# All norms of a two-block decoder kernel: reciprocal roots as one GpSimd power in place of a ScalarE, VectorE chain

## The chip, the cores and the metric

The kernel runs on one core of one Trainium2 chip. The metric is the device time of one execution in microseconds. TensorE does the matmuls, VectorE and ScalarE the elementwise work, GpSimd (called POOL in the profile) a few elementwise operations and some of the DMAs, SyncE the stream of weight loads.

## What is computed

A batch of 256 positions of width 2048 runs through two layers of a first model and two of a second. The part that matters here is how often a norm occurs:

```
for layer in range(2):                       # first block
    u = rmsnorm(h, norm_g[layer, 0])
    m = even_mixer(u) if layer == 0 else nsa_mixer(u)
    h = h + rmsnorm(m, norm_g[layer, 1])
    u = rmsnorm(h, norm_g[layer, 2])
    h = h + rmsnorm(swiglu(u), norm_g[layer, 3])
for layer in range(2):                       # second block
    h = rmsnorm(x, norm_g_2[layer])
    ...                                      # dilated + MoBA, then differential + stick-breaking
    x = x + y @ w_out[layer]
return rmsnorm(x, final_norm_g_2)
```

Each rmsnorm multiplies by (mean of squares + 1e-6) to the power -0.5. The even mixer has more: an L2 norm of the heads of q and k after a short convolution, and an rmsnorm of the heads of its two outputs. The differential attention has one on its output.

## The kernel before

The work has six stages, numbered 0 to 5: even mixer, SwiGLU, NSA mixer, SwiGLU, and the two layers of the second block. The 256 positions are two tiles of 128 partitions (t = 0, 1). Each weight is streamed from HBM in slots of 256 x 512 or 128 x 1024 elements, split by ScalarE into a high part (L1531, `WH`) and by VectorE into a low part (L1998, `WL`), and multiplied by TensorE three times (L1013 to L1015 for the columns of an input projection, L1060 to L1062 for the rows of an output projection). Three buffers hold split slots, so the split runs at most some slots ahead of TensorE.

All engines walk one list of steps, `ORDER`, written by `write_order`, and each engine does its own part of a step: `prep` is the split of a slot, `sq` and `stat` are sums of squares, `pre` is the norm ahead of a stage (its result `HR` scales what is drained from PSUM), `root` the norm of a stage's output (its result `MR` goes into `new_h`), `cv_r` and `cv_n` the L2 norm after the convolution, `og_r` and `og_m` the norm at the output gate of the even mixer, `y2d` that of the differential attention, `fin_s` and `fin_y` the last norm. An engine works its steps strictly in the order of the list: a step that waits holds all behind it on that engine.

A root is made by the helper `rstd`, which is in both the ScalarE and the VectorE program: VectorE writes x = mean + eps (L2005), ScalarE takes the square root (L1536), VectorE takes the reciprocal and one Newton step (L2007, L2009, L2011, L2013) and writes the result (L2015). The results lie in 24 columns each of a ring `RSQ`. The square root needs a table that most other functions don't share, so the compiler puts a table load ahead of a root and another ahead of the next function; a step `warm` (L1574) loads the table early, at the start of the second half of an output projection.

GpSimd's list has, besides elementwise steps, these DMAs, which matter below:

- `gb`: the row of gains of the coming output norm.
- `cm_w(0)` (L2595): the first half of the NSA compression weights, 2 MB, put in the list after the last step of stage 1's crossing into stage 2; it waits for the end of stage 1's matmuls alone. TensorE's `cm_h` (L1310) reads it.
- `tables_n` (L2586 to L2590): five tables of stage 2, about 1 MB. VectorE's and GpSimd's `cm_b` (L2280, L2604) wait for the last one and make the operand of `cm_h`.
- `tables_2` (L2621 to L2623): seven tables for stages 4 and 5, which wait for the residual stream of stage 4. Behind them stand a small operation (L2625), which waits for the last table, and `gb(4)`; then `rope` (L2633, L2634, L2637 on GpSimd, L2366, L2367, L2370 on VectorE), whose output TensorE's `feat` (L1407) reads.

`pre(2)` and `pre(4)` are put in the list by `cross`, ahead of these DMAs:

```
    ffn(1)              # ends with cross(1), which puts pre(2)
    put("cm_w", 0)
    put("tables_n")
    ...
    ffn(3)              # ends with cross(3), which puts pre(4)
    put("tables_2")
    put("gb", 4)
```

Of the kernel before, what the change touches and what calls it, by code (L numbers as in the profile page):

```python
# [21 lines left out]
EPS = 1e-6  # L22
# [221 lines left out]
def write_order(slots):  # L244
# [462 lines left out]
def build(nc, A, out):  # L707
    with ExitStack() as ctx:
# [30 lines left out]
        RSQ = sb("RSQ", 8 * 24)[:]  # L739
# [14 lines left out]
        one_b = SM[:, 30:31]  # L754

# [131 lines left out]
        rs_index = {}  # L887

        def rstd_of(w, *key):

            j = rs_index.setdefault(key, len(rs_index))
            before = [k for k, n in rs_index.items() if n == j - 8]
            return [RSQ[:, 24 * (j % 8) + 8 * i:24 * (j % 8) + 8 * i + w] for i in range(3)], before

# [14 lines left out]
        def slot_of(s):  # L909
# [3 lines left out]
            if wd < 64:  # L913
# [7 lines left out]
        a_hi, a_ut, a_ff, a_z, a_nm, a_gd, a_cv, a_hg, a_og, a_ns, a_b2, a_rs = (  # L921
            steps("s_act_" + n, act) for n in ("weights", "operand", "ffn", "sink", "norm", "gdn", "conv", "hgrn",
                                               "gate", "nsa", "block2", "root"))
# [3 lines left out]
        g_nm, g_gd, g_hg, g_og, g_ns, g_b2 = (  # L927
            steps("s_pool_" + n, pool) for n in ("norm", "gdn", "hgrn", "gate", "nsa", "block2"))
# [587 lines left out]
        def scalar(e):  # L1516
# [452 lines left out]
            def fin_s(t):  # L1969
# [17 lines left out]
        def vector(e):  # L1987
# [73 lines left out]
            def mul(st, c, t):  # L2061
# [3 lines left out]
                on.wait_ge(*v_rs.of("r", "pre", st))  # L2065
# [169 lines left out]
            def og_m(a, hf):  # L2235
                on.wait_ge(*v_rs.of("r", "og", a, hf))
# [203 lines left out]
            def y2d(i):  # L2440
# [7 lines left out]
                on.wait_ge(*v_rs.last())  # L2448
# [24 lines left out]
            def fin_y(t):  # L2473
                on.wait_ge(*v_rs.of("r", "pre", 6, t))
# [10 lines left out]
        def gpsimd(e):  # L2485
# [4 lines left out]


# [162 lines left out]
            def y2d(i):  # L2654
# [3 lines left out]
                e.tensor_tensor(sq, y, y, ALU.mult).then_inc(*g_b2.inc("sq", i))  # L2658
                on.wait_ge(*v_b2.of("yn", i))
# [109 lines left out]
```

## Time and profile before

| | us |
|---|---|
| median of 3 runs | 2965.33 |
| lowest and highest run | 2959.11, 2966.28 |
| the profiled execution | 2962.29 |
| its span, first to last instruction | 2960.5 |
| TensorE busy in the span | 2841.2 |
| VectorE busy | 1613.4 |
| ScalarE busy | 1402.6 |
| GpSimd busy | 234.6 |

The span is 1.8 us shorter than the execution's time. TensorE's busy time covers 96% of the span; its idle time, and the stretches in which the granted clock is at half, are all that a change off TensorE can alter. In rows of the timeline the numbers are start and duration in us, then engine, line, operation, tiles (out<-in) and form; in brackets stands how long the engine was idle ahead of the row and who ended that.

### The profile page before, as it was taken

To read this page: it belongs to the slowest core of one execution; us is meant where nothing else is said; L and a number is where in the kernel's file an instruction comes from. 1 tells how busy PE (TensorE), PEld (TensorE's weight loads), DVE (VectorE), ACT (ScalarE), POOL (GpSimd) and SP (SyncE) were. 2 spreads that over 40 slices of the span, in tenths; PEclk is the share of its full clock that TensorE was granted. 3 is DMA by queue.
4 is the path that set the end of the run, shared out by engine and by line. 5 is a ranking of instruction groups with operands and counts; after the bars stand their busy time and mean duration, and the time that the engine had idled before them with its cause. 6 is when DMAs were issued, how large, how long until landed. Compare 5 with 4: busy or idle time off the path is not lost.

```text
span 2960.5 us, 33218 instructions
## 1 busy us (share of the span) xinstructions
PE 2841.2 (96%) x13558; PEld 2346.8 (79%) x13558; DVE 1613.4 (54%) x2004; ACT 1402.6 (47%) x2045; POOL 234.6 (8%) x209
## 2 busy tenths in 40 slices
PE   8899999999999999999999999999999999999986
PEld 6787887777888888888888877788888888877765
DVE  5664666756554554444645545655455444476655
ACT  6554345546444444344544444644444434465563
POOL 0112332300000000000100101000000000011112
PEclk9999999999999999999999999999999999999998
DMA  6654543656666666555664423666666655554422
GB/s 211 123 115 120 106 106 85 122 180 192 185 192 191 185 191 191 187 191 190 192 190 138 140 95 129 191 185 192 191 185 190 191 188 191 190 182 143 135 93 99
DMA packets 212776, 480.85 MB, mean 162 GB/s; under 512 B 15248, under 2 KB 16272, under 8 KB 211984
## 3 DMA queue, kind: packets, MB, share of 16 engines
q1 hardware_dynamic: 210272, 467.57, 54.4%
q0 software_dynamic: 2352, 11.17, 1.1%
q8 instruction: 106, 1.74, 0.2%
q14 instruction: 46, 0.38, 0.0%
HBM read 476.58 MB, written 2.10 MB: 162 GB/s over the span
## 4 chain that ended last, share of the span: by engine, by line
PE 82%; DVE 8%; ACT 6%; issue 1%; POOL 1%; DMA 1%; SPq 0%; DVEq 0%; ACTq 0%; POOLq 0%
PE PS L1013 17%; PE PS L1015 17%; PE PS L1014 17%; PE PS L1062 7%; PE PS L1061 7%; PE PS L1060 7%; DVE WL L1998 2%; ACT WH L1531 1%; DVE WORK L2139 1%; PE PS L1171 1%; DVE XL L1998 1%; PE PS L1270 1%; PE PS L1359 1%; PE PS L1259 1%; PE PS L1086 1%
## 5 line engine op out<-in xcount | busy, mean ns | idle before, releaser
L1998 DVE TENSOR_TENSOR WL<-RAW,WH 128x1024 fp32r<-128x1024 f32 x827 | 1028.4, 1246 | 943.3 <-ACT WH L1531 942.3
L1531 ACT ACTIVATE WH<-RAW 128x1024 fp32r<-128x1024 f32 x831 | 874.5, 1054 | 849.3 <-PE PS L1015 524.0
L1013 PE MATMUL PS<-WH,UTH 128*128 128x512 f32 x2396 | 965.5, 403 | 25.0 <-DVE WL L1998 22.4
L1015 PE MATMUL PS<-WH,UTL 128*128 128x512 f32 x2396 | 939.9, 392 | 0.0
L1014 PE MATMUL PS<-WL,UTH 128*128 128x512 f32 x2396 | 939.3, 392 | 0.0
L1013 PEld LDWEIGHTS PS<-WH,UTH 128*128 128x128 f32 x2396 | 454.0, 189 | 124.7 <-DVE WL L1998 26.3
L1015 PEld LDWEIGHTS PS<-WH,UTL 128*128 128x128 f32 x2396 | 453.2, 189 | 98.4
L1014 PEld LDWEIGHTS PS<-WL,UTH 128*128 128x128 f32 x2396 | 454.4, 190 | 89.9 <-issue 1.9
L1062 PE MATMUL PS<-WH,HTL 128*128 128x512 f32 x656 | 259.3, 395 | 0.0
L1061 PE MATMUL PS<-WL,HTH 128*128 128x512 f32 x656 | 258.8, 394 | 0.0
L1060 PE MATMUL PS<-WH,HTH 128*128 128x512 f32 x656 | 255.4, 389 | 0.0
L1060 PEld LDWEIGHTS PS<-WH,HTH 128*128 128x128 f32 x656 | 125.3, 191 | 28.0
L1061 PEld LDWEIGHTS PS<-WL,HTH 128*128 128x128 f32 x656 | 123.2, 188 | 27.6
L1062 PEld LDWEIGHTS PS<-WH,HTL 128*128 128x128 f32 x656 | 123.2, 188 | 25.6
L1060 PE MATMUL PS<-WH,UTH 128*128 128x512 f32 x256 | 107.2, 419 | 4.1 <-DVE UTL L2041 4.0
L1061 PE MATMUL PS<-WL,UTH 128*128 128x512 f32 x256 | 103.9, 406 | 0.0
L1062 PE MATMUL PS<-WH,UTL 128*128 128x512 f32 x256 | 103.7, 405 | 0.0
L1998 DVE TENSOR_TENSOR XL<-RAW,XH 128x1024 fp32r<-128x1024 f32 x53 | 63.9, 1220 | 16.9 <-ACT XH L1531 16.9
L1580 ACT ACTIVATE BIG<-PS,SM 128x512 f32<-128x512 f32 x68 | 42.9, 683 | 51.0 <-PE PS L1015 50.7
L1552 ACT ACTIVATE UTH<-PS,GP 128x128 fp32r<-128x128 f32 x160 | 46.2, 386 | 41.8 <-PE PS L992 41.8
L1531 ACT ACTIVATE XH<-RAW 128x1024 fp32r<-128x1024 f32 x53 | 55.2, 1066 | 20.6 <-DMA RAW<-in_ffn_w_down 8.5
L1060 PEld LDWEIGHTS PS<-WH,UTH 128*128 128x128 f32 x256 | 50.9, 199 | 16.0 <-issue 3.2
(424 smaller groups left out, 2612.2 us busy)
## 6 DMA issues: line engine op xcount, KB each, us to landing
RAW<-in_ffn_w_gu SPq DMA_DIRECT2D x352, 512.0 KB, 4.2
RAW<-in_ffn_w_down SPq DMA_DIRECT2D x176, 512.0 KB, 4.4
RAW<-in_ab_w_in SPq DMA_DIRECT2D x128, 512.0 KB, 4.7
RAW<-in_nsa_w_in SPq DMA_DIRECT2D x80, 512.0 KB, 3.7
RAW<-in_w_in SPq DMA_DIRECT2D x64, 512.0 KB, 3.9
RAW<-in_ab_w_out SPq DMA_DIRECT2D x32, 512.0 KB, 4.4
RAW<-in_nsa_w_out SPq DMA_DIRECT2D x32, 512.0 KB, 3.8
RAW<-in_w_out SPq DMA_DIRECT2D x16, 512.0 KB, 3.8
```

Of the source, the lines that this page charges most:

```text
L1013: e.matmul(o, lh, wh[:, j], start=k + j == 0, stop=False)
L1014: e.matmul(o, lh, wl[:, j], start=False, stop=False)
L1015: x = e.matmul(o, ll, wh[:, j], start=False, stop=k + j == NKT - 1)
L1060: e.matmul(o, lh, wh[:, 0, cs], start=k == (0 if hf else LEFT[st][0]), stop=False)
L1061: e.matmul(o, lh, wl[:, 0, cs], start=False, stop=False)
L1062: x = e.matmul(o, ll, wh[:, 0, cs], start=False, stop=k == (KTILES[st] - 1 if hf else LEFT[st][-1]))
L1086: x = e.transpose(b[:, 128 * j:128 * j + 128], g[:, 128 * j:128 * j + 128], ident)
L1171: x = e.matmul(b[:, 128 * h:128 * h + 128], LTM[:, h], XX[:, h, 0], start=True, stop=True)
L1531: e.activation(wh, raw, ACTF.Copy).then_inc(*a_hi.inc(s))
L1552: e.activation(UTH[:, kk, 128 * t:128 * t + 128], b[:, 128 * j:128 * j + 128], ACTF.Copy, scale=GP[:, st, kk:kk + 1]).then_inc(*a_ut.inc(" ...
L1580: e.activation(dst, banks.ap("acc", st, c, t)[:, 0:WIDTHS[st][c]], ACTF.Copy, scale=HR[:, t:t + 1]).then_inc(*banks.empty(a_z, "acc", st, ...
L1998: e.tensor_tensor(wl, raw, wh.bitcast(F32), ALU.subtract).then_inc(*v_lo.inc(s))
```

## The change

`rstd` is gone from ScalarE. On VectorE it is one operation, which writes x over the sum itself, with the gain folded in. GpSimd raises it in place to the power -0.5, read from eight columns of constants (`MHALF`). The consumers wait for GpSimd's semaphore. GpSimd thereby gets the steps `pre`, `root`, `cv_r`, `og_r` and `fin_s`, and one operation in `y2d`; it does them where they stand in the list. The steps `warm` and the ring `RSQ` go away.

```diff
@@ right(st)
-        put("warm", "rows", st)
@@ scalar
-            def rstd(w, *key):
-                (x, y, z), before = rstd_of(w, *key)
-                on.wait_ge(*v_rs.of("x", *key))
-                e.activation(y, x, ACTF.Sqrt).then_inc(*a_rs.inc(*key))
...
-            @step
-            def pre(st):
-                rstd(2, "pre", st)
...
             def sink(dst, st, c, t, col):
                 on.wait_ge(*p_mm.of(col_end[st, c]))
-                on.wait_ge(*v_rs.of("r", "pre", st))
+                on.wait_ge(*g_rs.of("r", "pre", st))
@@ vector
             def rstd(o, ss, n, gain, *key):
-                (x, y, z), before = rstd_of(ss.shape[1], *key)
-                if before:
-                    on.wait_ge(*v_rs.of("r", *before[0]))
-                e.tensor_scalar(x, ss, 1.0 / n, EPS, ALU.mult, ALU.add).then_inc(*v_rs.inc("x", *key))
-                on.wait_ge(*a_rs.of(*key))
-                e.reciprocal(y, y).then_inc(*v_rs.inc("y", *key))
-                on.wait_ge(*v_rs.last())
-                e.tensor_tensor(z, y, y, ALU.mult).then_inc(*v_rs.inc("yy", *key))
-                on.wait_ge(*v_rs.last())
-                e.tensor_tensor(z, z, x, ALU.mult).then_inc(*v_rs.inc("xyy", *key))
-                on.wait_ge(*v_rs.last())
-                e.tensor_scalar(z, z, -0.5 * gain, 1.5 * gain, ALU.mult, ALU.add).then_inc(*v_rs.inc("z", *key))
-                on.wait_ge(*v_rs.last())
-                e.tensor_tensor(o, y, z, ALU.mult).then_inc(*v_rs.inc("r", *key))
+                e.tensor_scalar(o, ss, 1.0 / (n * gain * gain), EPS / (gain * gain), ALU.mult,
+                                ALU.add).then_inc(*v_rs.inc("x", *key))
...
             def new_h(st, t, n):
-                    on.wait_ge(*v_rs.of("r", "post", st, t))
+                    on.wait_ge(*g_rs.of("r", "post", st, t))
@@ gpsimd
+            def root_of(o, *key):
+                on.wait_ge(*v_rs.of("x", *key))
+                e.tensor_tensor(o, o, MHALF[:, 0:o.shape[1]], ALU.pow).then_inc(*g_rs.inc("r", *key))
+
+            @step
+            def pre(st):
+                root_of(HR, "pre", st)
...
             def y2d(i):
                 e.tensor_tensor(sq, y, y, ALU.mult).then_inc(*g_b2.inc("sq", i))
+                root_of(ST2[:, 64 + 4 * i:68 + 4 * i], "y2d", i)
                 on.wait_ge(*v_b2.of("yn", i))
```

The order of instructions shows what moves. GpSimd at the crossing from stage 1 to stage 2, before (the first row is `gb(1)`, the second `cm_w(0)`, the rest `tables_n` and the first of `cm_b`):

```order
L2508 DMA WORK<-in_norm_g 128x2048 [waits s_dve_norm]
L2595 DMA BIG<-in_nsa_cmp_w 128x32x128 [waits s_pe_weights]
L2586 DMA WORK<-in_pos 128x64 [waits s_act_norm,s_pe_weights,s_dve_norm]
L2587 DMA WORK<-in_nsa_cmp_w 128x2x128
L2588 DMA WORK<-in_c_db 128x1536
L2589 DMA SM<-in_c_dc 128x120
L2590 DMA SM<-in_c_mc 128x120
L2604 TENSOR_TENSOR BIG<-WORK 128x128 [waits s_dma_nsa_tables,s_act_nsa]
```

And after; `SM<-SM` are the powers, those of 128x1 for `root`, that of 128x2 for `pre(2)`:

```order
L2480 DMA WORK<-in_norm_g 128x2048
L2442 TENSOR_TENSOR SM<-SM 128x1 [waits s_dve_root] x2
L2442 TENSOR_TENSOR SM<-SM 128x2 [waits s_dve_root]
L2567 DMA BIG<-in_nsa_cmp_w 128x32x128 [waits s_pe_weights]
L2558 DMA WORK<-in_pos 128x64 [waits s_act_norm,s_pe_weights]
L2559 DMA WORK<-in_nsa_cmp_w 128x2x128
L2560 DMA WORK<-in_c_db 128x1536
L2561 DMA SM<-in_c_dc 128x120
L2562 DMA SM<-in_c_mc 128x120
L2576 TENSOR_TENSOR BIG<-WORK 128x128 [waits s_dma_nsa_tables,s_act_nsa]
```

Three operations that wait for VectorE now stand ahead of `cm_w(0)` and the tables. The same at the crossing from stage 3 to stage 4, before:

```order
L2508 DMA WORK<-in_norm_g 128x2048 [waits s_dve_norm]
L2621 DMA BIG<-in_c_r 128x128 [waits s_dve_norm]
L2621 DMA BIG<-in_c_r 128x64
L2621 DMA BIG<-in_c_lc 128x384
L2621 DMA BIG<-in_c_ca 128x384
```

and after:

```order
L2480 DMA WORK<-in_norm_g 128x2048
L2442 TENSOR_TENSOR SM<-SM 128x1 [waits s_dve_root] x2
L2442 TENSOR_TENSOR SM<-SM 128x2 [waits s_dve_root]
L2593 DMA BIG<-in_c_r 128x128
L2593 DMA BIG<-in_c_r 128x64
L2593 DMA BIG<-in_c_lc 128x384
L2593 DMA BIG<-in_c_ca 128x384
```

The seven DMAs of `tables_2` now stand behind `pre(4)`. ScalarE at the last output gate of stage 0 (`og_s`, L1756, and `og_q`, L1763), before:

```order
L1756 ACT_TABLE_LOAD
L1756 ACTIVATE BIG<-BIG 128x512 [waits s_act_sink] x2
L1558 ACTIVATE UTH<-PS 128x512 [waits s_pe_operand]
L1531 ACTIVATE WH<-RAW 128x1024 [waits s_dma_raw0]
L1763 ACTIVATE BIG<-BIG 128x512 x2
L1558 ACTIVATE UTH<-PS 128x512 [waits s_pe_operand]
L1531 ACTIVATE WH<-RAW 128x1024 [waits s_dma_raw1]
L1536 ACT_TABLE_LOAD
L1536 ACTIVATE RSQ<-RSQ 128x8 [waits s_dve_root]
L1558 ACTIVATE UTH<-PS 128x512 [waits s_pe_operand]
```

and after:

```order
L1725 ACTIVATE BIG<-BIG 128x512 [waits s_act_sink] x2
L1544 ACTIVATE UTH<-PS 128x512 [waits s_pe_operand]
L1522 ACTIVATE WH<-RAW 128x1024 [waits s_dma_raw0]
L1732 ACTIVATE BIG<-BIG 128x512 x2
L1544 ACTIVATE UTH<-PS 128x512 [waits s_pe_operand]
L1522 ACTIVATE WH<-RAW 128x1024 [waits s_dma_raw1]
L1544 ACTIVATE UTH<-PS 128x512 [waits s_pe_operand]
```

Both table loads and the square root are gone from this stretch. In the whole program the ScalarE table loads go from 53 to 29, and no other operation changes its place on ScalarE, VectorE or TensorE.

## Rows read from the trace of the kernel before

**Rows 1.** The page, part 1: busy time, share of the span and instructions.

```profile
PE 2841.2 (96%) x13558; PEld 2346.8 (79%) x13558; DVE 1613.4 (54%) x2004; ACT 1402.6 (47%) x2045; POOL 234.6 (8%) x209
```

**Rows 2.** Groups by line and form on ScalarE: busy us, mean ns | idle before.

```profile
L1536 ACT ACT_TABLE_LOAD x10 | 12.8, 1283 | 0.2
```

**Rows 3.** Timeline at the last norm: start, us, engine, line, operation, form.

```profile
2952.94 0.15 DVE L2005 TENSOR_SCALAR RSQ<-SM 128x1 f32<-128x1 f32 x1
...
2954.33 0.72 ACT L1980 ACTIVATE H<-H,SM 128x512 f32<-128x512 f32 x1 [1.00 <-DVE SM L2015]
```

**Rows 4.** Groups by line on GpSimd, columns as in Rows 2.

```profile
L2668 POOL TENSOR_TENSOR BIG<-BIG 128x128 f32<-128x128 f32 x8 | 4.7, 582 | 0.0
...
L2686 POOL MEMSET SM<- 128x1 f32 x1 | 0.1, 98 | 0.3 <-POOLq L2747 0.3
```

**Rows 5.** Timeline, stage 0, from the first columns to the last output gate.

```profile
42.01 0.50 PE L1013 MATMUL PS<-WH,UTH 128*128 128x512 f32 x1 [0.52 <-DVE WL L1998]
...
102.02 1.28 ACT L1694 ACT_TABLE_LOAD   x1
...
104.42 1.02 PE L1116 MATMUL PS<-MK,WORK 128*128 128x128 f32 x4 [2.82 <-ACT WORK L1694]
...
539.95 0.20 DVE L2007 RECIPROCAL RSQ<-RSQ 128x8 f32<-128x8 f32 x1 [2.83 <-ACT RSQ L1536]
...
544.32 0.46 PE L1285 MATMUL PS<-BIG,WORK 128*128 128x128 f32 x2 [1.24 <-DVE WORK L2271]
...
557.62 0.46 PE L1285 MATMUL PS<-BIG,WORK 128*128 128x128 f32 x2 [0.68 <-DVE WORK L2271]
...
586.06 0.46 PE L1285 MATMUL PS<-BIG,WORK 128*128 128x128 f32 x2 [1.37 <-DVE WORK L2271]
...
596.76 1.28 ACT L1756 ACT_TABLE_LOAD   x1
...
613.08 1.89 PE L1077 MATMUL PS<-MK,BIG 128*128 128x128 f32 x8 [4.70 <-POOL BIG L2565]
```

**Rows 6.** Timeline at the end, the attention of the last layer.

```profile
2901.04 1.09 PE L1077 MATMUL PS<-MK,BIG 128*128 128x128 f32 x4 [7.68 <-POOL BIG L2663]
...
2916.65 1.28 ACT L1910 ACT_TABLE_LOAD   x1
...
2926.55 0.63 PE L1077 MATMUL PS<-MK,BIG 128*128 128x128 f32 x4 [3.06 <-POOL BIG L2651]
```

**Rows 7.** Timeline into stage 2, and the landing of `cm_w` (last row).

```profile
1433.22 1.71 POOL L2595 DMA_DIRECT2D BIG<-in_nsa_cmp_w  x1 [726.23 <-PE PS L1062]
...
1458.80 0.17 DVE L2005 TENSOR_SCALAR RSQ<-SM 128x2 f32<-128x2 f32 x1
...
1459.16 0.55 POOL L2586 DMA_DIRECT2D WORK<-in_pos  x1 [24.23 <-DVE SM L2048]
...
1466.37 3.32 POOL L2604 TENSOR_TENSOR BIG<-WORK 128x128 f32<-128x128 f32 x7 [4.34 <-DMA SM<-in_c_mc]
...
1470.78 4.49 PE L1310 MATMUL PS<-BIG 128*128 128x60 f32 x39
...
DMA to landing us min/median/max: 11.5/12.2/12.9
```

**Rows 8.** Timeline into stage 4.

```profile
2629.74 1.07 POOL L2621 DMA_DIRECT2D BIG<-in_c_r  x2 [738.03 <-DVE H L2107]
...
2636.15 0.29 POOL L2625 TENSOR_SCALAR BIG<-BIG 128x128 f32<-128x128 f32 x1 [2.71 <-DMA BIG<-in_diff_lam]
...
2643.55 0.17 DVE L2005 TENSOR_SCALAR RSQ<-SM 128x2 f32<-128x2 f32 x1
...
2645.82 0.95 POOL L2633 TENSOR_TENSOR WORK<-BIG 128x256 f32<-128x256 f32 x1 [8.84 <-ACT BIG L1580]
...
2652.11 1.91 PE L1407 MATMUL PS<-MK,BIG 128*64 128x128 f32 x16 [0.85 <-DVE BIG L2370]
```

**Rows 9.** Windows: busy time (and instructions) of PE, PEld, DVE, ACT, POOL; clock; DMA.

```profile
2901.00:2907.00 6.00, 5.96 (x17) 4.88 (x18) 1.92 (x2) 1.55 (x2) 0.00 (x0) 0.51 0.37 117
```

More of the change, by code:

```diff
@@ L738, in build @@
         GP = sb("GP", 96)[:].rearrange("p (v k) -> p v k", v=6)
-        RSQ = sb("RSQ", 8 * 24)[:]
         HG = sb("HG", 128)[:]
@@ L754, in build @@
         one_b = SM[:, 30:31]
+        MHALF = SM[:, 504:512]
         def w3(o, n, a):
@@ L885, in operand_of @@
             return (ZN if st == 2 else Y2)[:, t, 128 * k:128 * k + 128]
[L887 to L893, printed above, removed]
         slots = weight_slots(A)
@@ L920, in build @@
             steps("s_pe_" + n, pe) for n in ("weights", "operand", "hidden", "gdn", "conv", "hgrn", "nsa", "block2"))
-        a_hi, a_ut, a_ff, a_z, a_nm, a_gd, a_cv, a_hg, a_og, a_ns, a_b2, a_rs = (
+        a_hi, a_ut, a_ff, a_z, a_nm, a_gd, a_cv, a_hg, a_og, a_ns, a_b2 = (
             steps("s_act_" + n, act) for n in ("weights", "operand", "ffn", "sink", "norm", "gdn", "conv", "hgrn",
-                                               "gate", "nsa", "block2", "root"))
+                                               "gate", "nsa", "block2"))
         v_lo, v_ut, v_ff, v_nm, v_gd, v_cv, v_hg, v_og, v_ns, v_b2, v_rs = (
@@ L926, in build @@
                                                "gate", "nsa", "block2", "root"))
-        g_nm, g_gd, g_hg, g_og, g_ns, g_b2 = (
-            steps("s_pool_" + n, pool) for n in ("norm", "gdn", "hgrn", "gate", "nsa", "block2"))
+        g_nm, g_gd, g_hg, g_og, g_ns, g_b2, g_rs = (
+            steps("s_pool_" + n, pool) for n in ("norm", "gdn", "hgrn", "gate", "nsa", "block2", "root"))
         d_raw = [steps(f"s_dma_raw{i}", by=16) for i in range(NRAW)]
@@ L1602, in z @@
                     on.wait_ge(*v_ut.of("acc", 0, c, 1))
-                    on.wait_ge(*v_rs.of("r", "pre", 0))
+                    on.wait_ge(*g_rs.of("r", "pre", 0))
                     S2 = v3(SPARE[0][:, 256:256 + 2 * (b - a)], 2)
@@ L1613, in n @@
                     on.wait_ge(*v_ut.of("acc", 2, c, 1))
-                    on.wait_ge(*v_rs.of("r", "pre", 2))
+                    on.wait_ge(*g_rs.of("r", "pre", 2))
                     S2 = v3(SPARE[2][:, 256:256 + 2 * (b - a)], 2)
@@ L1627, in gate @@
                 on.wait_ge(*p_mm.of(col_end[st, c]))
-                on.wait_ge(*v_rs.of("r", "pre", st))
+                on.wait_ge(*g_rs.of("r", "pre", st))
                 if q >= 2:
@@ L1708, in cv_r @@
             @step
-            def cv_r(hf, part):
-                rstd(8, "cv", hf, part)
-            @step
             def gd_b(hf, i):
@@ L1936, in y2d @@
             @step
-            def y2d(i):
-                rstd(4, "y2d", i)
-            @step
             def st_z(h):
@@ L1974, in fin_s @@
                                  accum_out=HSQ[:, 4 * t + n:4 * t + n + 1]).then_inc(*a_nm.inc("sq", 6, t, n))
-                rstd(1, "pre", 6, t)
             @step
             def fin_y(t):
-                on.wait_ge(*v_rs.of("r", "pre", 6, t))
+                on.wait_ge(*g_rs.of("r", "pre", 6, t))
                 e.activation(H[:, t, 1024:1536], H[:, t, 1024:1536], ACTF.Copy,
@@ L2064, in mul @@
                 on.wait_ge(*a_ff.of("acc", st, c - 1, t))
-                on.wait_ge(*v_rs.of("r", "pre", st))
+                on.wait_ge(*g_rs.of("r", "pre", st))
                 g = G[q % 2][t]
@@ L2161, in cv_n @@
                 c = 4096 + 1024 * part + 512 * hf
-                on.wait_ge(*v_rs.of("r", "cv", hf, part))
+                on.wait_ge(*g_rs.of("r", "cv", hf, part))
                 for t in range(2):
@@ L2235, in og_m @@
             def og_m(a, hf):
-                on.wait_ge(*v_rs.of("r", "og", a, hf))
+                on.wait_ge(*g_rs.of("r", "og", a, hf))
                 for i in range(2):
@@ L2447, in y2d @@
                 rstd(ss, ss, 64, 1.0 - LAMBDA, "y2d", i)
-                on.wait_ge(*v_rs.last())
+                on.wait_ge(*g_rs.of("r", "y2d", i))
                 e.tensor_tensor(y, y, bc(ss, 64), ALU.mult).then_inc(*v_b2.inc("yn", i))
@@ L2473, in fin_y @@
             def fin_y(t):
-                on.wait_ge(*v_rs.of("r", "pre", 6, t))
+                on.wait_ge(*g_rs.of("r", "pre", 6, t))
                 on.wait_ge(*d_gb.of(4))
@@ L2489, in step, with root, cv_r, og_r @@
                 do[f.__name__] = f
+            def root_of(o, *key):
[4 more added lines that the diff above has]
+                root_of(HR, "pre", st)
+            @step
+            def root(st, t):
+                root_of(MR[:, t:t + 1], "post", st, t)
+            @step
+            def cv_r(hf, part):
+                root_of(CSS[part], "cv", hf, part)
+            @step
+            def og_r(a, hf):
+                root_of(OSS[a][hf], "og", a, hf)
+            @step
+            def fin_s(t):
+                root_of(HR[:, t:t + 1], "pre", 6, t)
             def stream_made(st):
@@ L2684, in fin_y @@
                 e.tensor_tensor(H[:, t, 1024:1536], H[:, t, 1024:1536], GB[:, 1024:1536], ALU.mult).then_inc(*g_nm.inc("y", t, 2))
+            e.memset(MHALF, -0.5).then_inc(*g_nm.inc("mhalf"))
             e.memset(one_b, 1.0).then_inc(*g_nm.inc("one"))
+            on.wait_ge(*g_nm.of("mhalf"))
             for name, *a in ORDER:
```

10 lines of the change are left out of this document (removed).

## The prediction

> **What bounds the kernel now.** I read the page first: TensorE is busy for 2841.2 us of the 2960.5 us span, VectorE for 1613.4, ScalarE for 1402.6 and GpSimd for 234.6 [rows 1]. So some 119 us of TensorE idle time are all that a change on the other engines can touch, with the stretches at half clock. An operation saved on VectorE or ScalarE is worth something only where TensorE, or in the last few microseconds the chain to the output, waits for it. I therefore went to the timeline and took every gap ahead of a matmul in which a root or a table load stands. Those are in stage 0 [rows 5] and in the last layer's attention and final norm [rows 3, 6]. Then I looked where GpSimd's list changes: its DMAs at the two crossings [rows 7, 8].
>
> **What the change removes.** Of 53 ScalarE table loads 24 go, and 26 square roots. One load takes 1283 ns, and the ten ahead of a root had 0.2 us of idle time before them in all [rows 2]. So a load is worth 1.28 us where it is waited for. VectorE loses five small operations at each root. Most of this lies beside matmuls and is worth nothing. Call P the length of one power on GpSimd, handover aside. The places that count:
>
> - The first columns: TensorE waits 0.52 us for a split that the first root holds up [rows 5]: 0.5.
> - Matmul at 104.42, idle 2.82 us, released by ScalarE: the table load at 102.02 lies within that chain and has no reason left [rows 5]: 1.3.
> - Convolution norm: VectorE stands idle for 2.83 us until the square root is done, ahead of 539.95, and TensorE then has gaps of 1.24 and 0.68 us ahead of 544.32 and 557.62 [rows 5]. Without the loads and the square root both close: 1.9.
> - The gap of 1.37 us ahead of 586.06 has the same releaser [rows 5], and a root works up to it: 1.2 of it.
> - The gap of 4.70 us ahead of 613.08 [rows 5] follows the last output gate. The load at 596.76 goes (1.3), and the load and chain of its root shrink by about as much again: 2.6.
> - The gap of 3.06 us ahead of 2926.55 has the load at 2916.65 in its chain [rows 6]: 1.3.
> - Two roots of `y2d` and two of the final norm are chains that nothing covers. From the end of x (2952.94 plus 0.15) to the consumer at 2954.33 it is 1.24 us [rows 3]. Afterwards it is 0.1 for the handover, my allowance, plus P.
>
> P is in no row. GpSimd's shortest elementwise-like operation, a memset of one column, takes 98 ns, and a multiplication of 128 columns 582 ns [rows 4]. A power of 1 to 8 columns has the fixed part of these and some iteration inside. I take 0.5, near the second row. Nothing in the trace ends it upwards; I carry 0.1 to 2.3 (four times the 582 ns row). With P = 0.5 the last item is 4 x (1.24 - 0.1 - 0.5) = 2.6. The gains sum to 0.5 + 1.3 + 1.9 + 1.2 + 2.6 + 1.3 + 2.6 = 11.4 us; each microsecond more of P takes 4 back here.
>
> The Trainium skill (ScalarE: Activation LUTs, What ACT_TABLE_LOAD costs) puts a switch of tables at about 2.66 us, of which some 1.38 us are a drain. By that page each of the waited-for loads would give 1.4 more, and the sum would be about 17. The 0.2 us of idle time ahead of ten loads [rows 2] speaks against it here.
>
> **What the change adds.** GpSimd does the 26 powers in the order of its list, and it is idle for 92% of the span, so its own time is free. But an operation that waits holds up what is behind it. Ahead of `cm_w(0)` and `tables_n` stand now two `root` powers and that of `pre(2)`; ahead of `tables_2` the same for `pre(4)`.
>
> *Crossing into stage 2.* Before, `cm_w(0)` was issued at 1433.22, 25 us ahead of the tables at 1459.16 [rows 7], and landed 12.2 us later, long before anyone read it. Now it waits for the x of `pre(2)`, at 1458.80 plus 0.17, and for the power: it starts at 1458.97 + 0.1 + 0.5 = 1459.6. Its own issue takes 1.71 us, so the tables begin at 1461.3, and `cm_w(0)` lands at 1459.6 + 12.2 = 1471.8 [rows 7]. The tables stand in the same queue behind 2 MB. Before, `cm_b` was released at 1466.37, 7.2 us after the first table was issued; about 3 of these are five issues of 0.55 and more, so 4 are left behind `cm_w`'s landing: 1475.8. `cm_b` takes 3.32 us, and with handovers `cm_h` starts at 1479.5 in place of 1470.78 [rows 7]. That row has no idle time ahead, since TensorE was in other work, so cover is already counted: **+8.7**. Low end: if the tables don't wait for `cm_w`, they land 7.2 after 1461.3, at 1468.5, and with `cm_b` it is 1471.9, +1.1. High end: 12.9 for `cm_w`, and the 1 MB of tables at its rate (6.1): 1478.6, `cm_h` at 1482.1, +11.3.
>
> *Crossing into stage 4.* `tables_2` was issued at 2629.74, and its last table released GpSimd at 2636.15, 6.4 us later. Then GpSimd was idle for 8.84 us ahead of `rope` at 2645.82 [rows 8]: the old slack. Now the first table follows x at 2643.55 + 0.17 and the power: 2644.3. Landing 2650.7, the small operation 0.29 [rows 8], the issue of `gb(4)` 0.55 like a table's [rows 7]: `rope` starts at 2651.7, 5.9 late. TensorE's `feat` at 2652.11 had 0.85 us of idle time, released by that chain [rows 8], so there is no cover: **+5.9**, between 4 and 7.
>
> *The clock.* After an idle stretch of 7.68 us the matmuls from 2901.04 on [rows 6] ran with a granted clock of 0.51, that is at 1.2 GHz, for at least 6 us, though TensorE was busy 5.96 of them [rows 9]: half of 6, 3 us lost. Behind each of the two new gaps I expect the same in part and take 2 each, **+4**, between 0 and 6.
>
> GpSimd's other work: the powers of `cv_r` and `og_r` stand where GpSimd has little to do, and the later `gb` rows are read long after; I cost both at nothing, covered by GpSimd's 92% idle time.
>
> **The sum** against the profiled execution (span 2960.5, time 2962.29): -11.4 + 8.7 + 5.9 + 4 = +7.2 at P = 0.5, 2969.5. Each microsecond of P adds 4 to the chains and 2 at the crossings. The median of the runs is 3.0 above that execution; on it, 2965.33 + 7.2 = 2972.5, rounded 2973.0.
>
> **Rivals.**
>
> 1. *The power is dear* (P of 1.5 to 2.3). For: a root of a power has to be computed with something, and no row of this trace shows such a function on GpSimd. Against: at most 8 columns. It adds 6 to 11: 2979 to 2984, slower. It decides from P about 0.8, where the loss passes 8.9 us.
> 2. *The tables overtake `cm_w(0)`, or the table DMAs go quicker.* For: DMA queues have 16 engines, which are not full. Then the first crossing costs 1.1 and its clock nothing: -11.4 + 1.1 + 5.9 + 2 = -2, 2963.
> 3. *Neither delay binds.* Then the gain stands alone: 2954, faster. For: VectorE's and ScalarE's lists get shorter just there, and x may come earlier. Against: x follows the sums of squares of the residual stream, which TensorE's outputs set, not the root of old.
> 4. *The first power pays for code that isn't there.* No row shows a cost like it: GpSimd's memset took 98 ns with 0.3 idle before it [rows 4]. If the first power took ten times the 128-column row, 5.8 us, the drains of the first columns would wait for it; with half of it covered by the free PSUM banks it is +3: 2976.
>    The Trainium skill (GPSIMD Engine Reference, Instruction dispatch) says that the first call into a newly loaded GpSimd kernel takes about 6 us, without an instruction of its own in the profile.
> 5. *A load hides more than its own time*, so that every switch on the path gives twice as much. Four loads or so are on the path: 4 x 1.28 = 5.1 more gain, net +2: 2967.
>    The drain of the page named above would do that.
> 6. *The change doesn't do what it says*: the order of instructions shows the loads gone and every power in its place, so I give that nothing.
>
> **Chances.** Forecast (net +2 to +13) 0.50; dear power 0.17; tables overtake 0.13; neither binds 0.08; first call 0.07; loads worth twice 0.05. A measurement of this kernel tells about 0.3% from no change, 8.9 us here. Of the forecast 0.29 lies within that and 0.21 above. Faster: nearly all of rival 3, and a little of 2 and 5, 0.10. Within: 0.29 and most of 2 and 5, and a little of 4, 0.46. Slower: 0.21, all of 1, most of 4, 0.44. The range must take in P up to 2.3 and the low crossing of rival 2, and leaves out rival 3 and the tails: 2963 to 2985.
>
> **What would show it.** Powers on GpSimd of about 0.5 us, each starting 0.1 after its x. 29 table loads on ScalarE. The first row of `cm_w(0)` near 1460 less what stage 0 gained, landing 12 us later, and a gap of some 8 us ahead of `cm_h`, with GpSimd idle ahead of `cm_b` until a table lands. A gap of 6 us ahead of `feat` in stage 4, with rows at half clock behind both. The gaps of stage 0 smaller by the terms above; x to consumer in the last norm near 0.6 us. I am wrong if `cm_h` starts within 2 us of where the rest of the timeline puts it, if powers take over 1 us, or if stage 0 gains much more or less than 7.5 us.

## The result and the profile after

| | before | after |
|---|---|---|
| median of 6 runs each, us | 2962.16 | 2972.47 |
| the profiled execution | 2962.29 | 2972.49 |
| its span | 2960.5 | 2970.7 |

The ratio of after to before is 1.0036, with a 95% interval of 1.0026 to 1.0047: the kernel became slower, by 10.3 us. The prediction was 2973.0. The sum behind it was +7.2 on a baseline median of 2965.33, which with three more runs came to 2962.16; so the time was met more closely than the difference, 7.2 against 10.3. That the two times agree within 0.5 us is luck: the first median lay 3.2 us above the later one.

The page, part 1, of the kernel after (answers to [rows 1]):

```profile
PE 2847.1 (96%) x13558; PEld 2354.3 (79%) x13558; DVE 1593.1 (54%) x1874; ACT 1369.8 (46%) x1989; POOL 262.3 (9%) x236
```

VectorE is 20 us less busy, ScalarE 33 us less, GpSimd 28 us more, and none of this is the result. TensorE, with the same 13558 matmuls, is 6 us more busy: the same work at a lower clock. Its idle time (the span less the busy time) went from 119.3 to 123.6 us.

The powers, in the groups by line and form of GpSimd (busy us, mean ns | idle before), after:

```profile
L2442 POOL TENSOR_TENSOR SM<-SM 128x8 f32<-128x8 f32 x8 | 14.9, 1866 | 81.4 <-DVE SM L1962 81.4
...
L2442 POOL TENSOR_TENSOR SM<-SM 128x1 f32<-128x1 f32 x10 | 5.6, 557 | 1608.2 <-DVE SM L1962 1608.2
...
L2442 POOL TENSOR_TENSOR SM<-SM 128x2 f32<-128x2 f32 x6 | 4.3, 709 | 165.5 <-DVE SM L1962 165.5
...
L2442 POOL TENSOR_TENSOR SM<-SM 128x4 f32<-128x4 f32 x2 | 2.0, 1012 | 1.5 <-DVE SM L1962 1.5
```

A power is 0.56 us for one column, and each further column costs 0.15: 0.71 for two, 1.01 for four. Of those of eight columns six took 1.64 or 1.65 us and two 2.54. I had taken 0.5 for all.

TensorE's instructions are the same in both kernels and in the same order, so the start of one matmul in both timelines gives a running account of what was won and lost up to it. The rows of after on which it rests (for [rows 5] to [rows 8]):

```profile
101.11 0.66 PE L1107 MATMUL PS<-MK,WORK 128*128 128x128 f32 x4 [1.43 <-ACT WORK L1667]
...
539.06 0.46 PE L1276 MATMUL PS<-BIG,WORK 128*128 128x128 f32 x2 [0.16 <-DVE WORK L2219]
...
604.26 1.94 PE L1068 MATMUL PS<-MK,BIG 128*128 128x128 f32 x8 [2.72 <-POOL BIG L2537]
...
1452.11 1.09 PE L1291 MATMUL PS<-MK,BIG 128*128 128x128 f32 x8
...
1469.20 6.20 PE L1301 MATMUL PS<-BIG 128*128 128x60 f32 x28 [7.79 <-DVE BIG L2228]
...
1505.53 1.66 PE L1301 MATMUL PS<-BIG 128*128 128x60 f32 x13 [0.53 <-issue]
...
2665.58 2.74 PE L1398 MATMUL PS<-MK,BIG 128*64 128x128 f32 x12 [7.04 <-POOL BIG L2609]
...
2756.72 0.63 PE L1068 MATMUL PS<-MK,BIG 128*128 128x128 f32 x4 [1.90 <-POOL BIG L2623]
...
2937.74 0.63 PE L1068 MATMUL PS<-MK,BIG 128*128 128x128 f32 x4 [1.65 <-POOL BIG L2623]
```

Three anchors of before that stand in no group yet, from its timeline:

```profile
1461.62 1.09 PE L1300 MATMUL PS<-MK,BIG 128*128 128x128 f32 x8 [0.49 <-ACT BIG L1580]
...
1498.05 2.22 PE L1310 MATMUL PS<-BIG 128*128 128x60 f32 x18 [0.52 <-issue]
...
2741.69 0.63 PE L1077 MATMUL PS<-MK,BIG 128*128 128x128 f32 x4 [1.89 <-POOL BIG L2651]
```

| matmul | before | after | difference | step |
|---|---|---|---|---|
| operand after the last output gate, stage 0 | 613.08 | 604.26 | -8.8 | -8.8 |
| first transposes in stage 2 | 1461.62 | 1452.11 | -9.5 | -0.7 |
| first `cm_h` | 1470.78 | 1469.20 | -1.6 | **+7.9** idle |
| second `cm_h` | 1498.05 | 1505.53 | +7.5 | **+9.1** half clock |
| `feat`, stage 4 | 2652.11 | 2665.58 | +13.5 | **+6.0** idle |
| operand, end of stage 4 | 2741.69 | 2756.72 | +15.0 | **+1.6** half clock |
| operand, end of stage 5 | 2926.55 | 2937.74 | +11.2 | -3.8 |
| end of the span | 2960.5 | 2970.7 | +10.2 | -1.0 |

So the change won 14 us in stage 0, stage 5 and at the end, and lost 25 at the two crossings. Not all of the 14 us is idle time that went; some 5 us of it are shown further down to be something else. GpSimd's timeline at the first crossing, after:

```profile
1449.73 0.17 DVE L1962 TENSOR_SCALAR SM<-SM 128x2 f32<-128x2 f32 x1
...
1449.98 0.71 POOL L2442 TENSOR_TENSOR SM<-SM 128x2 f32<-128x2 f32 x1 [19.70 <-DVE SM L1962]
...
1450.64 1.75 POOL L2567 DMA_DIRECT2D BIG<-in_nsa_cmp_w  x1
...
1465.70 3.25 POOL L2576 TENSOR_TENSOR BIG<-WORK 128x128 f32<-128x128 f32 x7 [10.42 <-DMA SM<-in_c_mc]
```

GpSimd waits 19.70 us for x; behind it the 2 MB go out, then the tables. The 2 MB landed at 1462.3 and the last table at 1465.6, 3.3 us later; it releases `cm_b` at 1465.70, 15.1 us after `cm_w(0)` was issued, and TensorE waits 7.79 us. The windows of after (columns as in [rows 9]) then show the clock:

```profile
1469.00:1477.00 8.00, 7.80 (x37) 7.83 (x37) 2.37 (x3) 0.00 (x0) 0.00 (x0) 0.50 0.16 49
1477.00:1485.00 8.00, 8.00 (x34) 7.61 (x34) 1.56 (x4) 1.17 (x2) 1.61 (x1) 0.50 0.01 2
1485.00:1493.00 8.00, 8.00 (x31) 6.42 (x31) 2.33 (x3) 1.70 (x3) 0.11 (x1) 0.80 0.88 310
```

and the first of these windows before:

```profile
1469.00:1477.00 8.00, 8.00 (x66) 7.68 (x64) 3.12 (x4) 1.65 (x2) 0.69 (x2) 1.00 0.18 49
```

In 8 us TensorE did 37 matmuls at a granted clock of 0.50 (1.2 GHz) where it had done 66 at 1.00.

### The profile page after: what moved, and what is told of

It reads as the page before. It is cut to its first block, busy times and chain, and to the rows that moved or that the text cites. A ratio compares the mean times of both kernels' runs of the same rounds, so it can differ in the third digit from the quotient of the medians.

```text
span 2970.7 us, 33059 instructions
## 1 busy us (share of the span) xinstructions
PE 2847.1 (96%) x13558; PEld 2354.3 (79%) x13558; DVE 1593.1 (54%) x1874; ACT 1369.8 (46%) x1989; POOL 262.3 (9%) x236
## 4 chain that ended last, share of the span: by engine, by line
PE 84%; DVE 6%; ACT 6%; POOL 2%; DMA 1%; issue 1%; SPq 0%; DVEq 0%; ACTq 0%; POOLq 0%
PE PS L1004 17%; PE PS L1006 17%; PE PS L1005 17%; PE PS L1051 7%; PE PS L1052 7%; PE PS L1053 7%; DVE WL L1958 2%; ACT WH L1522 1%; DVE WORK L2087 1%; PE PS L1261 1%; PE PS L1162 1%; PE PS L1350 1%; PE PS L1301 1%; PE PS L1250 1%; PE PS L1077 1%
## 5 line engine op out<-in xcount | busy, mean ns | idle before, releaser
L1958 DVE TENSOR_TENSOR WL<-RAW,WH 128x1024 fp32r<-128x1024 f32 x827 | 1029.0, 1246 | 957.5 <-ACT WH L1522 956.5
L1004 PEld LDWEIGHTS PS<-WH,UTH 128*128 128x128 f32 x2396 | 454.3, 190 | 124.0 <-DVE WL L1958 25.5
L2442 POOL TENSOR_TENSOR SM<-SM 128x1 f32<-128x1 f32 (+3 forms) x26 | 26.8, 1030 | 1856.5 <-DVE SM L1962 1856.5
```

Of the source, the lines that this page charges most:

```text
L1004: e.matmul(o, lh, wh[:, j], start=k + j == 0, stop=False)
L1958: e.tensor_tensor(wl, raw, wh.bitcast(F32), ALU.subtract).then_inc(*v_lo.inc(s))
```

## The experiments

My theory: the powers themselves gain some 14 us, mostly through table loads, and the DMAs that now stand behind powers lose more. All experiments ran beside the kernel before (median 2960.7 to 2960.9 us).

### The DMAs put ahead of the powers: dma_first

```diff
@@ cross(st)
             if j == 5:
+                if st == 1:
+                    put("cm_w", 0)
+                if st == 3:
+                    put("tables_2")
                 put("pre", st + 1)
@@
-    put("cm_w", 0)
     put("tables_n")
@@
-    put("tables_2")
     put("gb", 4)
```

> The changed kernel, with cm_w(0) put into GpSimd's list ahead of the power of pre(2), and tables_2 ahead of that of pre(4); nothing else. Theory (the DMAs stood behind powers that wait for VectorE): in the timeline of the changed kernel TensorE lost 16.7 us around cm_h (7.9 of idle time, the rest at half clock) and 7.3 us around feat in stage 4. Both go: 2972.5 - 24 = 2948.5 us, about 0.995 of the kernel before, no gap of over 1 us ahead of cm_h or ahead of feat of stage 4. Rival (the place of the DMAs doesn't matter, the crossings are late because the norm's result comes later from GpSimd): the gaps stay, 2972.

Measured: 2950.73 us, ratio to before 0.9968 (0.9955 to 0.9980). The two starts, in TensorE's timeline:

```profile
1464.93 7.36 PE L1303 MATMUL PS<-BIG 128*128 128x60 f32 x64 [1.08 <-DVE BIG L2230]
...
2644.03 1.91 PE L1400 MATMUL PS<-MK,BIG 128*64 128x128 f32 x16 [0.20 <-DVE BIG L2320]
```

The 7.79 and 7.04 us of idle time are 1.08 and 0.20, and all 64 of the `cm_h` matmuls took 7.36 us, where 28 took 6.20 in the kernel after. The rival is out, and the same powers with the DMAs in another place make the kernel faster than before. 1.08 is slightly over the 1 us that I allowed; sm_first below takes it away.

### One crossing alone: cmw_first

The edit is dma_first without the two lines for stage 3, and `tables_2` where it was.

> The changed kernel, with cm_w(0) alone put ahead of the power of pre(2); tables_2 stays behind that of pre(4). Theory: the gap ahead of cm_h goes, the gap of 7.0 us ahead of feat in stage 4 stays: 2972.5 - 16.7 = 2955.8 us. Rival (the five small tables, not the 2 MB ahead of them, are what comes late): they are still issued after the power, so cm_b starts late and at least half of the 7.8 us gap stays, 2965 or more.

Measured: 2960.57 us, ratio 1.0001 (0.9992 to 1.0010). The gap ahead of `cm_h` shrank from 7.79 to 1.13 us, that ahead of `feat` is there:

```profile
1466.30 1.89 PE L1302 MATMUL PS<-BIG 128*128 128x60 f32 x15 [1.13 <-DVE BIG L2229]
...
2654.54 3.25 PE L1399 MATMUL PS<-MK,BIG 128*64 128x128 f32 x16 [6.68 <-POOL BIG L2610]
```

The two crossings are separate losses. In time, moving `cm_w(0)` gives 11.9 and moving `tables_2` another 9.8, where I had split them 16.7 to 7.3. The crossings themselves fit better than the medians: by the starts of the same matmuls moving `cm_w(0)` gave back 15.7 us around `cm_h`, and moving `tables_2` 7.7 around `feat`. Elsewhere other things moved: a gap of 1.9 us in stage 0 that both reordered kernels had and the kernel after had not (told in the last section), and stretches at half clock, such as one near 1814 us that cmw_first had and dma_first had not, worth 2.4 us. The rival is out: the small tables are issued after the power here too, and with the 2 MB out of their way they are in time.

### The delay alone in the kernel before: late_dma

```diff
@@ gpsimd, kernel before
+            @step
+            def root(st, t):
+                on.wait_ge(*v_rs.of("x", "post", st, t))
+
+            @step
+            def pre(st):
+                on.wait_ge(*v_rs.of("x", "pre", st))
```

> The kernel before, with its square roots, and GpSimd only made to wait for VectorE's x of every root and pre where the changed kernel has the powers: no power is computed. This puts the delay of the DMAs alone into the kernel before. Theory: it loses what the changed kernel loses at the crossings, less the 0.7 us that the power takes at each: 2962.2 + 24 - 1.4 = 2984.8 us, gaps of about 7 and 6 us ahead of cm_h and feat. Rival (the power itself, or its result coming late, makes the gaps): 2962, as before.

Measured: 2991.18 us, ratio 1.0107 (1.0091 to 1.0122), the profiled execution 2987.7 (span 2985.9). Its `cm_h` and `feat`:

```profile
1477.39 3.00 PE L1310 MATMUL PS<-BIG 128*128 128x60 f32 x13 [7.79 <-DVE BIG L2280]
...
2673.91 2.31 PE L1407 MATMUL PS<-MK,BIG 128*64 128x128 f32 x10 [7.35 <-POOL BIG L2645]
```

Without a single power the gaps are as in the kernel after: a wait in GpSimd's list is all it takes. The loss is 25.4 us in the span and 30.5 in the medians, against 22.6 expected. I had taken 0.7 us off each gap for the missing power, and that was wrong: the DMAs began 0.67 us after the end of x (1458.31 against 1457.64) where with the power it was 0.74 (1450.64 against 1449.90). The rest of the excess lies behind the second gap, at half clock (by the starts of the same matmuls 8.5 us behind the first gap and 3.8 behind the second, where the kernel after had 9.1 and 1.6).

### The table loads put back: switches

On dma_first, ScalarE gets its square roots and `warm` again, of a constant into a column that nobody reads:

```diff
@@ scalar, on dma_first
+            def rstd(*key):
+                on.wait_ge(*g_nm.of("one"))
+                on.wait_ge(*v_rs.of("x", *key))
+                e.activation(SM[:, 31:32], one_b, ACTF.Sqrt).then_inc(*a_nm.inc("rt", *key))
...
+            @step
+            def pre(st):
+                rstd("pre", st)
```

> dma_first (2950.7 us), with ScalarE's square roots put back where they stood, of a constant column into a column that nobody reads, and warm: the table loads go from 29 back to 53, while the powers stay on GpSimd and nobody waits for a square root. It still waits for VectorE's x, as before. Theory (the gain in stage 0 and ahead of the last output operand comes from table loads in ScalarE's chain): the gaps ahead of L1116, L1276 and L1068 come back in part, 1.3 + 1.2 + 1.2 + 2 in stage 0 and 1.3 at the end, +7: 2957.7 us, with 1.28 us for each load that is waited for. Rival (the gain comes from the shorter chain of the root itself): +1 or less, 2951. Rival (a switch costs a drain of as much again): each of these gaps grows by 2.6 and not by 1.3, 2964.

Measured: 2962.06 us, ratio to before 1.0008 (0.9997 to 1.0020), 11.3 us above dma_first. The gaps of stage 0 and of the end are back (the first row is ScalarE's, in the chain of the second):

```profile
102.74 1.28 ACT L1700 ACT_TABLE_LOAD   x1
...
105.14 1.11 PE L1110 MATMUL PS<-MK,WORK 128*128 128x128 f32 x4 [2.82 <-ACT WORK L1700]
...
545.44 0.46 PE L1279 MATMUL PS<-BIG,WORK 128*128 128x128 f32 x2 [1.29 <-DVE WORK L2253]
...
615.62 1.94 PE L1071 MATMUL PS<-MK,BIG 128*128 128x128 f32 x8 [4.57 <-POOL BIG L2571]
...
2930.22 0.63 PE L1071 MATMUL PS<-MK,BIG 128*128 128x128 f32 x4 [3.06 <-POOL BIG L2657]
```

They are 2.82, 1.29, 4.57 and 3.06 us; before it was 2.82, 1.24, 4.70 and 3.06 [rows 5, 6]. So the gain comes with ScalarE's part of the root, and not with the shorter chain of the root itself. This kernel has the powers, all the loads and the DMAs in time, and it takes what the kernel before takes: as a way to make a root, a power on GpSimd is worth nothing that can be measured here. The run puts back the loads and the square roots together. Where a load stands directly ahead of the operation that TensorE waits for, and no square root near it (102.74 above, and 2920.32 at the end), the gain is the load; in stage 0's other chains the two aren't told apart.

I expected +7 and got +11.3. TensorE's idle time, 119.1 us against 112.0 in dma_first, grew by 7.1, as expected, with 1.05 us of it ahead of the first columns (at 42.75), which I had not named. The rest, in the profiled executions, is half clock, and most of that isn't the loads' doing. One stretch, from 1504 on, cost some 5 us; the only idle time close ahead of it is a gap of 0.53 us (ahead of 1501.39), and sm_first below has the same gap (ahead of 1489.41) and stays at 1.00. The window in switches:

```profile
1502.00:1512.00 10.00, 10.00 (x60) 10.00 (x58) 1.23 (x1) 0.99 (x2) 0.00 (x0) 0.62 0.19 54
```

Each gap grew by about one load: from 1.39, 0.16, 2.70 and 1.65 us in dma_first, by 1.43, 1.13, 1.87 and 1.41 us. The Trainium skill (ScalarE: Activation LUTs, What ACT_TABLE_LOAD costs) gives 2.66 us for a switch with its drain; the trace doesn't agree here, it shows the load of 1283 ns and, at the first gap, 0.15 us more.

### Each power twice: pow_twice

```diff
@@ gpsimd, on dma_first
             def root_of(o, *key):
                 on.wait_ge(*v_rs.of("x", *key))
+                e.tensor_tensor(SCR[:, 0:o.shape[1]], o, MHALF[:, 0:o.shape[1]], ALU.pow)
                 e.tensor_tensor(o, o, MHALF[:, 0:o.shape[1]], ALU.pow).then_inc(*g_rs.inc("r", *key))
```

> dma_first (2950.7 us), with every power made twice in a row on GpSimd, the first time into a scratch of eight columns that nobody reads. Each power takes as much again: 0.56 us (one column), 0.71 (two), 1.01 (four), 1.64 (eight). Theory (only chains that nothing covers pay for the length of a power): two of y2d and two of the final norm, 2 x 1.01 + 2 x 0.56 = 3.1, and about 1.5 at the convolution norm, whose gap of TensorE was only just closed: +3 to +6, about 2955 us. Rival (powers are on the path everywhere): the 26 durations sum to 26.8 us, 2977. Rival (none is): 2951.

Measured: 2959.67 us, ratio to before 0.9996 (0.9987 to 1.0004), 8.9 us above dma_first. GpSimd's busy time grew by 28.7 us (290.0 against 261.3), and a third of that is on the path, more than I thought and far less than all. Where:

```profile
610.80 1.32 PE L1071 MATMUL PS<-MK,BIG 128*128 128x128 f32 x8 [4.28 <-POOL BIG L2541]
...
1460.60 1.09 PE L1294 MATMUL PS<-MK,BIG 128*128 128x128 f32 x8 [1.66 <-ACT BIG L1560]
...
2654.45 1.91 PE L1401 MATMUL PS<-MK,BIG 128*64 128x128 f32 x16 [1.74 <-DVE BIG L2321]
...
2903.47 1.09 PE L1071 MATMUL PS<-MK,BIG 128*128 128x128 f32 x4 [9.31 <-POOL BIG L2640]
```

The gaps were 2.70, 0.10, 0.20 and 7.31 in dma_first. So the power of the last output gate costs its full 1.6 us (8 columns), `y2d` its 2 x 1.0, and the convolution norm 1.5 (new gaps of 0.70 and 0.78 us ahead of 502.39 and 584.77), as expected. The norms ahead of stages 2 and 4 cost about 1.5 each; those two I had priced through the DMAs alone, and missed that TensorE's first transposes and `feat` wait for the drains that `HR` scales. Twice their own 0.71 it is because the second power of two columns ran beside a split of VectorE, and took 1.58 us where the first, at 1456.91, took 0.72 (at 2645.94 it was 1.59):

```profile
1457.40 1.23 DVE L1961 TENSOR_TENSOR WL<-RAW,WH 128x1024 fp32r<-128x1024 f32 x1 [0.58 <-ACT WH L1525]
...
1457.61 1.58 POOL L2446 TENSOR_TENSOR SM<-SM 128x2 f32<-128x2 f32 x1
```

### What the clock did in the gap: fill, fill_all, fill_wide

All three are the kernel after, with matmuls of the identity put ahead of the first `cm_h`, into the bank that `cm_h` overwrites.

```diff
@@ tensor, cm_h(part), fill
-                b = take("cm_h", part)[:, 0:60]
+                b = take("cm_h", part)
+                if part == 0:
+                    for l in range(27):
+                        e.matmul(b[:, 0:128], ident, ident, start=True, stop=True)
+                b = b[:, 0:60]
```

In fill_all the count is 34; in fill_wide it is 8 matmuls of `ident` with `H[:, 0, 0:512]`.

> The changed kernel, with 27 matmuls of 128x128 of the identity put ahead of the first cm_h, into the PSUM bank that cm_h overwrites: about 7 us of work (1.02 us for 4) in the 7.8 us gap. Theory (cm_h and what follows ran at half clock because TensorE was idle): the clock stays at full, cm_h takes 0.11 us a matmul in place of 0.21, and 5.7 us come back: 2966.8 us. Rival (cm_h is slow for another reason, such as weights that landed just before): cm_h stays at 0.21 a matmul, 2972.

Measured: 2971.67 us, ratio to before 1.0031 (1.0020 to 1.0043).

> fill with 34 matmuls of the identity in place of 27. In fill they took 6.19 us at full clock, and an idle time of 1.51 us was left ahead of cm_h; the clock fell to half in the course of cm_h. 34 take 7.8 us and leave none. Theory (idle time of TensorE alone brings the clock down): with no idle time left the clock stays at full through cm_h and behind it, and the 8.8 us that the changed kernel loses at half clock there come back: 2972.5 - 8.8 = 2963.7 us. Rival (something else in that stretch, such as the short matmuls themselves, brings it down): it falls as in fill, 2971.

Measured: 2964.93 us, ratio 1.0018 (1.0009 to 1.0028).

> The same gap of the changed kernel filled with 8 matmuls of the identity with 512 columns of the residual stream (some 7 us in all) in place of 27 with 128 columns. Theory (idle time alone): as fill, which left 1.5 us of idle time and half clock from the middle of cm_h on, 2971. Rival (what kind of matmuls fill the gap matters): the clock stays at full further into or through cm_h, and up to 8.8 us come back, 2963.7.

Measured: 2971.34 us, ratio 1.0038 (1.0023 to 1.0052).

TensorE's timeline, of fill:

```profile
1464.70 6.19 PE L1299 MATMUL PS<-MK 128*128 128x128 f32 x54
1472.40 3.88 PE L1305 MATMUL PS<-BIG 128*128 128x60 f32 x25 [1.51 <-DVE BIG L2232]
```

of fill_all:

```profile
1462.26 7.75 PE L1299 MATMUL PS<-MK 128*128 128x128 f32 x68
...
1470.07 7.36 PE L1305 MATMUL PS<-BIG 128*128 128x60 f32 x64
```

and of fill_wide:

```profile
1462.09 7.03 PE L1299 MATMUL PS<-H,MK 128*128 128x512 f32 x16
...
1469.90 10.42 PE L1305 MATMUL PS<-BIG 128*128 128x60 f32 x58 [0.78 <-DVE BIG L2232]
```

With no idle time left (fill_all) `cm_h` takes 7.36 us, as at full clock, the granted clock is 1.00 in every window of the stretch, and 7.5 us of the medians come back, 8.9 of the profiled executions; 8.8 was expected. That settles that the 9.1 us of the table above are the clock and that a filled gap avoids them; the delay of the DMAs itself stays. What it doesn't settle is how little idle time is enough. With 1.51 us (fill) and with 0.78 us (fill_wide) the clock still fell in the course of `cm_h`: the windows of 8 us show 0.83, 0.50 and 0.82 from 1469 on in fill, and 0.58 and 0.57 from 1471 on in fill_wide. In dma_first, with 1.08 us ahead of `cm_h` and other matmuls before that, it stayed at 1.00. (The profiled execution of fill_wide took 2980.6 us, 9 more than its median, with more stretches at half clock later on.) So idle time right ahead isn't the whole condition. Whether it is what TensorE did in the stretch before, or the moment at which the idle time falls, I have no run that separates; the stretch from 1504 in switches shows that the clock can fall in one execution and not in another behind the same gap. The runs of fill reach from 2966.4 to 2972.3 us, and only the slowest of them was profiled, so in some executions the 27 matmuls may have kept the clock up.

### The best version: sm_first

```diff
@@ gpsimd, on dma_first
+            @step
+            def tables_sm():
+                stream_made(2)
+                e.dma_start(SM[:, 200:320], A["c_dc"]).then_inc(*d_ntab.inc("dc"))
+                e.dma_start(SM[:, 320:440], A["c_mc"]).then_inc(*d_ntab.inc("mc"))
...
-                e.dma_start(SM[:, 200:320], A["c_dc"]).then_inc(*d_ntab.inc("dc"))
-                e.dma_start(SM[:, 320:440], A["c_mc"]).then_inc(*d_ntab.inc("all"))
@@ cross(st), st == 1
                     put("cm_w", 0)
+                    put("tables_sm")
```

> dma_first (2950.7 us), with the two small tables c_dc and c_mc, which go to SM, issued right behind cm_w(0), ahead of the power of pre(2); the three into WORK stay behind it. In dma_first the last table landed at 1461.2 and TensorE still had a gap of 1.1 us ahead of cm_h. Theory: two issues of 0.54 us fewer between the power and the last landing, cm_b starts 1.1 us or a little more earlier, the gap goes, 2949.6 us; next late is nothing, since the gap was all. Rival (the bandwidth of the 0.8 MB table and not the issues sets the last landing): less than 0.5 us.

Measured: 2949.46 us, ratio to before 0.9959 (0.9947 to 0.9971). `cm_h`:

```profile
1462.16 6.05 PE L1304 MATMUL PS<-BIG 128*128 128x60 f32 x53
```

`cm_h` has no idle time ahead any more. Of the 2.8 us by which it starts earlier than in dma_first, 1.1 is this gap; the rest stems mostly from the gap of 1.9 us in stage 0, which this execution had not. The medians differ by 1.3 us, less than both intervals allow to tell apart. It is the fastest of all versions, 11 us or 0.4% below the kernel before.

## Why the prediction was nearly right

- **The places of gain** were the right ones, and priced a little too high. The gap at 104.42 shrank from 2.82 to 1.43, those ahead of 544.32, 557.62 and 586.06 to 0.16 and nothing, that ahead of 613.08 from 4.70 to 2.72. Another 0.7 came by the drains of stage 2. In stage 5 the gap ahead of 2926.55 shrank from 3.06 to 1.65. By the starts of the matmuls it is -8.8 against -7.5 forecast in stage 0, -4.8 against -3.9 in stage 5 and at the end, and 14.3 against 11.4 in sum. But TensorE's idle time grew by 4.3 us in all; with the 13.9 of the two new gaps taken off, 9.6 us of it went, where the forecast was 11.4. The other 4.7 us are in no term of the forecast, and so luck. About 1 us came ahead of the first root (late_dma, which has the roots of before, has 0.9 of it too), and most of the rest because stretches at half clock that the kernel before had elsewhere were shorter or missing. One example is this stretch of the same work, first in before, then in after:

```profile
2799.00:2809.00 10.00, 7.17 (x42) 5.27 (x43) 4.82 (x6) 4.58 (x9) 1.36 (x2) 0.83 0.34 107
...
2813.00:2823.00 10.00, 7.55 (x51) 5.80 (x51) 5.61 (x9) 4.83 (x12) 1.70 (x2) 1.00 0.34 107
```

  That the reason for the gaps was ScalarE's part, with its table loads, is shown by switches.
- **The last norm**: from the end of x to the consumer it was 1.24 us [rows 3], it became 0.67:

```profile
2963.76 0.15 DVE L1962 TENSOR_SCALAR SM<-SM 128x1 f32<-128x1 f32 x1
2963.99 0.56 POOL L2442 TENSOR_TENSOR SM<-SM 128x1 f32<-128x1 f32 x1 [3.72 <-DVE SM L1962]
2964.58 0.72 ACT L1940 ACTIVATE H<-H,SM 128x512 f32<-128x512 f32 x1 [1.05 <-POOL SM L2442]
```

  That is 0.57 a norm, against 0.64. For `y2d`, at 1.01 us a power, it was about 0.1 each (the gap ahead of 2901.04 went from 7.68 to 7.39), since P isn't one number but grows with the columns. The range of P held all its values but the 2.54 us of two powers. One of the prediction's own signs of being wrong was a power of over 1 us, and ten of the 26 are: the sum put P only on chains of one to four columns, and left out that the last output gate has one of 1.64 us in its chain. That gap gave 2.0 us in place of 2.6.
- **The delays**: +7.9 and +6.0 against +8.7 and +5.9. The working held in its steps: the last table released `cm_b` 15.1 us after `cm_w(0)` was issued, where 12.2 + 4 = 16.2 was said.
- **The clock** is the term that was mis-sized: 4 us, with 6 as its upper end, against 9.1 + 1.6 = 10.7. I took a stretch of 6 us at half clock from [rows 9], which costs 3, and put 2 behind each gap. After the first crossing's gap it lasted far longer: by the three windows of after, 16 us at 0.50 and 8 at 0.80, so 8 + 1.6 = 9.6 us lost by that count. The row showed that the clock falls and not how long it stays down, and a bound from one window of 6 us was no upper end. These 6.7 us too little and the 4.7 us of luck above, with the small misses of the other terms, cancel in part: the difference was missed by 3.1 us, and the clock alone by more than twice that.
- **Rivals.** The tables don't overtake the 2 MB; both delays bind; powers are not dear, at 0.56 to 1.64 us on the chains. A load didn't hide more than its own time: switches has 1.13 to 1.87 us a gap, not twice 1.28. The first power took 0.71 us, as every one of two columns in this execution, so its own time shows no cost of a first call; the Trainium skill (GPSIMD Engine Reference, Instruction dispatch) has about 6 us for code that is newly loaded, and no run here shows it for this operation.

## What to carry to other kernels

When an operation that waits is given to an engine that also issues DMAs, read what stands behind it in its list: the powers themselves cost little here, and the DMAs behind them 25 us. Put DMAs that depend on little ahead of operations that wait for a late value; the same change with two lines moved is 0.3% faster than the original instead of 0.36% slower. Price an idle gap of TensorE at the gap plus the stretch at half clock behind it, which can be the larger part; and look for the gain of such a change in the table loads that it removes from a waited-for chain, not in the busy time. Before a gain or loss of some 3 us is explained, compare the granted clock of the two executions window by window: a stretch at half clock more or less was worth 1.5 to 5 us here.

## What the runs showed of the hardware

A GpSimd power costs about 0.40 us plus 0.15 us for each of its columns (0.56, 0.71 and 1.01 for 1, 2 and 4; 1.64 for most of 8).

GpSimd and VectorE take longer side by side (the power of 1.58 us in pow_twice is one case), and which one pays can change though the operations are the same. VectorE's split of a slot (L1998 before) takes 1246 ns in the mean. Near 541 us in stage 0, in dma_first, it was this:

```profile
541.02 3.89 POOL L2539 TENSOR_TENSOR BIG<-BIG 128x512 f32<-128x512 f32 x2 [2.65 <-DVE BIG L2189]
...
541.46 4.53 DVE L1960 TENSOR_TENSOR WL<-RAW,WH 128x1024 fp32r<-128x1024 f32 x2
...
546.64 1.55 PE L1252 MATMUL PS<-WC,BIG 128*128 128x512 f32 x3 [1.89 <-DVE WORK L2213]
```

and in the kernel after, with the same operations in the same order at that place:

```profile
540.79 5.15 POOL L2537 TENSOR_TENSOR BIG<-BIG 128x512 f32<-128x512 f32 x2 [2.66 <-DVE BIG L2187]
...
541.23 2.36 DVE L1958 TENSOR_TENSOR WL<-RAW,WH 128x1024 fp32r<-128x1024 f32 x2
```

Once GpSimd takes 3.89 us and VectorE 4.53 for two splits, and TensorE waits 1.89; once it is 5.15 and 2.36, and TensorE doesn't wait. Of the profiled executions, those of dma_first, cmw_first, pow_twice and switches had this gap, and those of the kernel after, sm_first and the three fills had not; with one profile for each, I can't say whether it goes with the execution or with the program. The Trainium skill (GPSIMD Engine Reference, Specifications) says that GpSimd shares its SBUF interfaces with VectorE and collides with its instructions that have two SBUF inputs; the split is one of these, and the rows above agree with it, though no run here takes the one engine's work away to show that the other is then fast.
